# One fp32 transformer pair on one core: residual merge a chunk earlier, ones matmuls inside half blocks, fewer table loads, ScalarE for the high parts of entry blocks

## What is computed

```python
# first block
mix = concatenate([y_pool, y_sb]) @ w_out
h = h + rms_norm(mix, g_mix_post)
m = square(relu(rms_norm(h, g_mlp_pre) @ w_up)) @ w_down      # 4096 wide
h = h + rms_norm(m, g_mlp_post)
h = h + sigmoid(h @ w_ple_gate) * rms_norm(p @ w_ple_proj, g_ple)
# second block; sh, sc, g are columns of c_act @ w_ada + b_ada
x = h
x = x + g_m * hybrid_mixer(modulate(rmsnorm(x, norm_mix_g), sh_m, sc_m))
x = x + g_f * conv_ffn(modulate(rmsnorm(x, norm_ffn_g), sh_f, sc_f))   # silu(gate)*val @ w_down, 2816 wide
out = rmsnorm(x, norm_final_g)
```

## Time and profile before

| | us |
|---|---|
| median of 3 runs | 3202.91 |
| lowest, highest | 3197.24, 3203.24 |
| profiled execution, own time | 3209.44 |
| its span in the trace | 3207.7 |
| PE busy | 2999.0 (93%) |
| DVE, POOL, ACT busy | 1600.0, 1056.6, 796.3 |

### The profile page before, as it was taken

How to read it: one execution, slowest core, us unless ns; L and a number is a source line. 1 busy time by engine, 2 the same in 40 slices (tenths; PEclk the granted TensorE clock), 3 DMA queues, 4 the chain that set the end, 5 groups by cost and what they waited for, 6 DMA issues and landing times. The chain is left out here.

```text
span 3207.7 us, 34389 instructions
## 1 busy us (share of the span) xinstructions
PE 2999.0 (93%) x13294; PEld 2380.5 (74%) x13294; DVE 1600.0 (50%) x1598; ACT 796.3 (25%) x1066; POOL 1056.6 (33%) x476
## 2 busy tenths in 40 slices
PE   6999998999999998989999796799998999999996
PEld 5876576788888886768887564677786888888885
DVE  3639946545555557741300566555546433343337
ACT  2138843211222113220021234133213111111112
POOL 2330032444444442433343211310243343343441
PEclk9999999999999999989999697789999999999998
DMA  2121031122232222121122330200321111111111
GB/s 104 52 67 27 3 143 46 53 91 93 92 105 92 93 91 92 40 100 51 54 109 95 86 74 30 63 14 14 142 95 44 48 46 52 46 46 52 46 47 64
DMA packets 69593, 216.37 MB, mean 67 GB/s; under 512 B 9088, under 2 KB 15488, under 8 KB 68736
## 3 DMA queue, kind: packets, MB, share of 16 engines
q1 hardware_dynamic: 65616, 200.48, 19.6%
q10 hardware_dynamic: 3888, 14.68, 1.1%
HBM read 170.50 MB, written 22.54 MB: 60 GB/s over the span
## 5 line engine op out<-in xcount | busy, mean ns | idle before, releaser
L278 POOL TENSOR_TENSOR w_hi<-w_raw,inv_count 128x1024 fp32r<-128x1024 f32 x202 | 389.9, 1930 | 1780.3 <-PE ps L303 1113.2
L281 POOL TENSOR_TENSOR w_lo<-w_raw,w_hi 128x1024 fp32r<-128x1024 f32 x202 | 533.1, 2639 | 15.9
L303 PE MATMUL ps<-x_hi,w_hi 128*128 128x512 f32 x1216 | 378.7, 393 | 16.0 <-POOL w_lo L281 9.9
L303 PE MATMUL ps<-x_lo,w_hi 128*128 128x512 f32 x1216 | 377.1, 391 | 0.0
L303 PE MATMUL ps<-x_hi,w_lo 128*128 128x512 f32 x1216 | 377.0, 391 | 0.0
L303 PEld LDWEIGHTS ps<-x_hi,w_hi 128*128 128x128 f32 x1216 | 230.2, 190 | 65.9 <-issue 11.9
L303 PEld LDWEIGHTS ps<-x_lo,w_hi 128*128 128x128 f32 x1216 | 230.3, 189 | 48.3
L303 PEld LDWEIGHTS ps<-x_hi,w_lo 128*128 128x128 f32 x1216 | 229.9, 189 | 48.2
L303 PE MATMUL ps<-hidden_hi,w_hi 128*128 128x512 f32 x800 | 247.6, 391 | 11.7 <-DVE residual L2955 11.7
L303 PE MATMUL ps<-hidden_hi,w_lo 128*128 128x512 f32 x800 | 247.2, 390 | 0.0
L303 PE MATMUL ps<-hidden_lo,w_hi 128*128 128x512 f32 x800 | 247.2, 390 | 0.0
(11 more groups left out here) (399 smaller groups left out, 5078.5 us busy)
## 6 DMA issues: line engine op xcount, KB each, us to landing
w_raw<-wall SPq DMA_DIRECT2D x221, 512.0 KB, 3.5
ada_raw<-wada SPq DMA_DIRECT2D x48, 512.0 KB, 4.2
gates_scratch<-gate_out ACTq DMA_DIRECT2D x16, 512.0 KB, 2.6
gate_in<-gates_scratch SPq DMA_DIRECT2D x8, 1024.0 KB, 8.5
residual<-x_t SPq DMA_DIRECT2D x8, 512.0 KB, 8.6
residual<-x_t SPq DMA_DIRECT2D x2, 2048.0 KB, 9.6
emb_scratch<-emb_out ACTq DMA_DIRECT2D x8, 512.0 KB, 2.6
embedding<-emb_scratch SPq DMA_DIRECT2D x2, 2048.0 KB, 12.5
```

The lines of the kernel that those rows point to most:

```text
L278: nc.gpsimd.tensor_tensor(w_hi[:, slot, :], w_raw[:, slot, :], one.to_broadcast([P, S]), ALU.mult).then_inc(w_split, 1)
L281: nc.gpsimd.tensor_tensor(w_lo[:, slot, :], w_raw[:, slot, :], w_hi[:, slot, :].bitcast(F32), ALU.subtract).then_inc(w_split, 1)
L303: last = nc.tensor.matmul(ps[:, banks + c, :], lhs, x[:, k0 + k, c * HALF:(c + 1) * HALF], start=(left == nk * 3 - 1), stop=(left == 0))
```

## The change

1. **Merge** (mlp2_vector): the 8 instructions that add `acc2` to the residual move from behind `hidden` of the last chunk to in front of it, right behind the down sums of the chunk before; their wait on `pair_free` goes from 116 to 112.
2. **Ones matmul of half 0** moves from behind block (half 1, first of two) into it: behind its fourth tile in out1 and out2, behind its sixth in gate.
3. **Table loads**: three loads by hand are gone (start of mlp1, in2 and mlp2), one is put in gate behind the sigmoids of half 0. The last sigmoid piece of block GG + 6 and what hangs on it (`gate_last`, `gate_square`, `gate_add`, `gate_sum`) move from gate into in2.
4. **High parts**: for the first two blocks of mlp1, gate, in2 and mlp2 (8 blocks of 221), ACT makes w_hi (`split_high`) and POOL only w_lo (`split_low`).

```diff
+    def split_low(pool, b):
+        slot = b % 2
+        pool.wait_ge(w_split, b * 2 + 1)
+        nc.gpsimd.tensor_tensor(w_lo[:, slot, :], w_raw[:, slot, :],
+                                w_hi[:, slot, :].bitcast(F32), ALU.subtract).then_inc(w_split, 1)
+
+    def split_high(act, b):
+        slot = b % 2
+        act.wait_ge(w_landed[slot], 16 * (b // 2 + 1))
+        act.wait_ge(w_split, 2 * b)
+        act.wait_ge(w_used, b + 1)
+        nc.scalar.activation(w_hi[:, slot, :], w_raw[:, slot, :], ACT.Identity).then_inc(w_split, 1)
...
-    def last_two(pe, g0, x_hi, x_lo, job, between):
+    def last_two(pe, g0, x_hi, x_lo, job, between, at):
                 for k in range(8):
+                    if (c, u, k) == (1, 0, at):
+                        between()
                     last = half_step(pe, (g0 + u) % 2, x_hi, x_lo, k, 2 * u + c, c)
                 last.then_inc(half_full.sem if c == 0 else w_used, 1)
-                if (c, u) == (1, 0):
-                    between()
...
     def mlp1_scalar(act):
-        load_exp_ln()
...
         act_half_rstd(act, 0, 1)
         gain = lambda k: C1("g_mlp_pre", k)
+        split_high(act, GM)
         residual_high(act, 0, 0, gain)
...
         for k in range(1, 8):
             residual_high(act, k, 0, gain)
+            if k == 1:
+                split_high(act, GM + 1)
...
     def gate_scalar(act):
         square(11)
+        split_high(act, GG)
         for k in range(8):
             residual_high(act, k, 0)
             if k < 4:
                 square(12 + k)
+            if k == 3:
+                split_high(act, GG + 1)
...
     def in2_vector(dve):
         with before(GATE):
+            dve.wait_ge(*pair_free.at(7))
+            gate_add(dve, 6, 9, 1)
             dve.wait_ge(*pair_free.at(8))
             gate_add(dve, 7, 10, 1)
...
     def mlp2_vector(dve):
             down(4, 0)
-            hidden(*chunk_args(4, 1))
-            dve.wait_ge(*pair_free.at(116))
+            dve.wait_ge(*pair_free.at(112))
             for k in range(8):
                 nc.vector.scalar_tensor_tensor(out=res2[:, k, :], in0=acc2[:, k, :], scalar=ada_col(5, k),
                                                in1=res2[:, k, :], op0=ALU.mult, op1=ALU.add).then_inc(merged.sem, 1)
+            hidden(*chunk_args(4, 1))
             dve.wait_ge(*merged.at(8))
             down(4, 1, True)
```

More of the change, by code:

```diff
@@ L1083, in out1_pool @@
     def out1_pool(pool):
-        split_blocks(pool, GO + 2, GM + 1)
+        split_blocks(pool, GO + 2, GM)
+        split_low(pool, GM)
     def out1_scalar(act):
@@ L1214, in out1_tensor @@
                     pe.wait_ge(*pair_free.at(14 + u - 1))
-                last = out1_tiles((b + u) % 2, u, range(8), (c,), True, True)
-                last.then_inc(half_full.sem if c == 0 else w_used, 1)
                 if (c, u) == (1, 0):
+                    out1_tiles((b + u) % 2, u, range(4), (c,), True, False)
                     pe.wait_ge(*square_added.at(8 + 8))
                     half_stat(pe, 0).then_inc(stat_full.sem, 1)
+                    last = out1_tiles((b + u) % 2, u, range(4, 8), (c,), False, True)
+                else:
+                    last = out1_tiles((b + u) % 2, u, range(8), (c,), True, True)
+                last.then_inc(half_full.sem if c == 0 else w_used, 1)
     def out1_vector(dve):
@@ L1356, in mlp1_pool @@
     def mlp1_pool(pool):
-        split_blocks(pool, GM + 1, GM + 64)
+        split_low(pool, GM + 1)
+        split_blocks(pool, GM + 2, GM + 64)
     def square_sum(dve, n):
@@ L1606, in gate_pool @@
     def gate_pool(pool):
-        split_blocks(pool, GG, GI + 1)
+        split_low(pool, GG)
+        split_low(pool, GG + 1)
+        split_blocks(pool, GG + 2, GI)
+        split_low(pool, GI)
     def gate_square(act, k, c=None):
@@ L1663, in stat_0 @@
             half_stat(pe, 0).then_inc(stat_full.sem, 1)
-        last_two(pe, GG + 6, x_hi, x_lo, 6, stat_0)
+        last_two(pe, GG + 6, x_hi, x_lo, 6, stat_0, 6)
     def gate_sum(dve, k, n, c=None):
@@ L1756, in in2_pool @@
     def in2_pool(pool):
-        split_weights(pool, GI, 34)
+        split_low(pool, GI + 1)
+        split_blocks(pool, GI + 2, GI + 35)
     def in2_scalar(act):
@@ L1769, in in2_scalar @@
         with before(GATE):
+            gate_last(act, 0)
             gate_last(act, 1)
+        load_exp_ln()
+        split_high(act, GI + 1)
+        with before(GATE):
+            gate_square(act, 6, 1)
         high(2, 0)
@@ L1825, in in2_vector @@
         with before(GATE):
+            dve.wait_ge(*pair_free.at(7))
+            gate_add(dve, 6, 9, 1)
             dve.wait_ge(*pair_free.at(8))
             gate_add(dve, 7, 10, 1)
+        low(1, 0)
         scaled(2, 0)
-        low(1, 0)
+        with before(GATE):
+            gate_sum(dve, 6, 9, 1)
+        scaled(3, 0)
+        low(2, 0)
         with before(GATE):
             gate_sum(dve, 7, 10, 1)
-        for k in range(3, 8):
+        low(3, 0)
+        for k in range(4, 8):
             scaled(k, 0)
-            low(k - 1, 0)
+            if k > 4:
+                low(k - 1, 0)
         low(7, 0)
@@ L2671, in out2_pool @@
     def out2_pool(pool):
-        split_weights(pool, GY, 8)
+        split_blocks(pool, GY + 1, GN)
+        split_low(pool, GN)
     def out2_tensor(pe):
@@ L2787, in mlp2_pool @@
     def mlp2_pool(pool):
-        split_weights(pool, GN, 66)
+        split_low(pool, GN + 1)
+        split_blocks(pool, GN + 2, W_TOTAL)
     def final_square(act, n):
```

14 lines of the change are left out of this document (5 added, 9 removed).

## The result

The changed kernel takes 3183.08 us (median of 5 runs, 3178.80 to 3187.89) against 3202.91. The ratio is 0.9942 with a 95% interval from 0.9924 to 0.9961: 18.6 us faster, between 12.5 and 24.3. Forecast were 25.2 us and 3177.7; the time lies inside the stated range, and the gain is a quarter smaller than the sum. The profiled execution is the median one, with a span of 3181.3 us.

The account below looks back on a forecast made before the run. PE, busy 2999.0 of 3207.7 us, was taken as the bound, so only its stops and half clock pay. Terms of 14.7 + 1.0 + 1.5 + 7.0 + 1.0 = 25.2 us off the 3202.9 median gave 3177.7, range 3168 to 3188.

Parts of the forecast that it names:

- Term 1: Last chunk: moving the merge removes PE's stop and the half clock behind it; -14.7 us, between -13 and -15.5.
- Rival C: Last chunk: the merge meets POOL's weight passes and is not hidden, so PE waits; gain 14.5 us, 3188.4; chance 0.03.
- Term 4: Entry of in2: nothing stands before Ln any more, so Ln of half 1 comes earlier; -7.0 us, from -5 to -9.
- Terms 2 and 5: Entries of mlp1 and mlp2: earlier start, then held by second w_lo; -1.0 us each, to 0 or -2.7 and -2.2.
- Term 3: Entry of gate: PE starts 4.5 us earlier, then waits for the second block's w_lo; -1.5 us, from +0.3 to -3.4.
- B: Entries: later w_lo eats the gains; mlp1, gate, mlp2 give nothing, in2 only 3; gain 17.7 us, 3185.2; chance 0.17.
- A: Entries: shorter gaps bring the clock back to 2.4 GHz, each entry takes its outer value; gain 31.9 us, 3171.0; chance 0.17.
- D: Entries: first blocks fed in drips keep the clock at 1.2 GHz, kernel slower than before, 3207.7 us; chance 0.02.

Follow-up runs that it names:

- e2_no_merge: The changed kernel with the merge put back in its old place, all four entries as changed; 3198.96 us, ratio 0.9981.
- e4_gate_second_sooner: The changed kernel with one line moved: in gate's entry ScalarE makes the second block's high part after x_hi of tile 2, ahead of square 14; 3174.29 us, ratio 0.9914.
- e5_vector_low: On top of e4_gate_second_sooner, VectorE makes the second block's low part in all four entries, and mlp1's high part comes one tile sooner; 3180.54 us, ratio 0.9930.

## Why the prediction was right, and where not

- **Term 1, -14.7: right.** The changed kernel's trace gives 14.7 and the merge alone gives 14.7 by its trace and 15.0 by the ratio. Both traces are set against the same profiled execution before; against e2_no_merge's, where half clock behind the stop was shorter, it is 13.4, still inside the range of 13 to 15.5. The merge was slower than reckoned (16.05 us for 13.38) and so made the convolution later than the 2.3 us forecast: it ended at 3094.31, and the account puts the old start of that step, 3101.00, at 3089.34, so 5.0 us. It ended as forecast in the next idle time. Rival C was right that the merge would meet POOL's passes (2.7 us more) and wrong that PE would see it.
- **Term 4, -7.0: right in mechanism, a little large.** Three executions with these entries give -5.6 to -6.6, 6.2 in the mean. Less the account of -1.97, the forecast places were 1364.7 for tile 1 (1364.92 in the trace), 1369.5 for tile 2 (1369.68) and 1372.9 to 1375.8 for Ln of half 1 (1375.25). The clock took the slow end.
- **Terms 2 and 5, -1.0 each: -0.3 and -0.6 in the mean of three executions (+0.2 to -0.7, and -0.5 to -0.6).** PE starts as much sooner as said (2.7 us in mlp1 for 2.8, 3.1 in mlp2 for 3.2). The step that was off is who holds it afterwards: not PE's own wait for w_lo but a DVE instruction on the way to tile 1, which w_lo blocks (2.84 and 2.85 us). Among the signs, a wait for w_lo was to be PE's longest in mlp1 and mlp2; the rows name x_lo and y_lo, so that sign failed in both and came true in gate alone.
- **Term 3, -1.5: wrong, +0.2 to +0.5.** The places agree up to the hold (PE's first tile 4.9 us earlier, forecast 4.5; w_lo of the second block done at 1259.35, forecast 1260.9 less 2.04, so 0.5 late). The step that failed is the one behind: "five half steps of 0.68 us and two ones matmuls lead to Ln of half 1", 4.6 us at full clock and 6.5 with part of it at half. At full clock the same stretch took 5.53 (e4_gate_second_sooner), and 7.65 in the changed kernel. Five half steps are 3.4 us, so the working leaves 1.2 for the two ones matmuls. The rows show more. The first takes 0.46 us itself, but from the start of the matmul behind it to the next are 0.64 us instead of 0.23 at full clock (1266.46 to 1267.10) and 1.22 instead of 0.43 at half (1261.77 to 1262.99), so it costs 0.87 at full clock. Behind the second, which starts at 1266.01, Ln starts at 1267.06, 1.05 us later. Together 1.9 instead of 1.2. The rest is clock: the first two half steps with their ones matmul took 4.43 us (1259.41 to 1263.84) against 2.33 in e4_gate_second_sooner; from there to Ln both took 3.2.
- **The rivals.** B named the cause, the second block's w_lo, and its price was right for gate; for in2 it took away too much (3 left, 6.2 measured). By the total its 17.7 us are nearer to the measured 18.6 than the forecast's 25.2, which lies outside the interval of the gain. The time fell inside the stated range because that was drawn to take in B. A's half, the clock, was put as a gain that might come of itself with shorter stops (its value for in2 is 8.8 by the forecast's own places, not 8.9). It did not come: in all four entries half clock stood behind the last of the stops that were left (2.31, 4.50, 3.79 and 3.00 us), and with the clock kept up gate, in2 and mlp2 gave 2.1 + 1.6 + 1.5 us more. D never came near: these 5.2 us are far from the 25.2 that half clock would have had to cost.
- **The sum.** In the entries 6.8 us by the mean of the executions (0.3 + 6.2 + 0.6 less 0.3), where the forecast had 10.5. That is all that was missing: 14.7 + 6.8 = 21.5 (20.2 with the merge at 13.4), which the measured interval of 12.5 to 24.3 holds and the 25.2 of the forecast doesn't.
- **Against which execution.** Taking the differences off the median and not off the profiled execution was right: its own 3209.44 was 6.5 us above the median, and outside the four entries and the last chunk the other traces are 0.7 to 12.1 us shorter than it (difference of the spans less the sum of the table).

## What to carry to other kernels

When a wait at the start of a stage is taken away, look for the next block's preparation: it was hidden by that wait, and if it is queued in a fixed place on its engine it becomes the new stop; moving one line was worth 5.2 us in the trace, where all changes to the entries together had given 6.8. A stop of a few microseconds is paid twice where the clock falls behind it, so cheap work for PE in the stop can give back what no reordering does. And for terms of 1 to 5 us, compare one instruction's start in two traces stage by stage: the totals of the whole kernel scatter by more. Take several executions for that too: a single entry differed by up to 1.5 us between two executions of the same instructions.

## What the runs showed of the hardware

- Throwaway matmuls in the stops held the granted clock at 1.00 through gate, in2 and mlp2, where it was 0.83 to 0.89, and through mlp1 (0.83) in one of two executions; in the other it was 0.94. In gate PE went on at the same instant with them, by the account, as without.
- The same stop of 2.42 us, in code that both kernels share, was followed at once by half clock in two of the twelve traces here (the changed kernel and e5_vector_low) and by full clock in the other ten. Such places may account for the differences of up to 12.1 us between executions in untouched stages. What decides it in each was not tried.
- Behind a ones matmul (its operands are read as fp32, those of the products as fp32r) the next matmul runs 0.41 us longer from start to start at full clock, 0.8 at half, and the Ln that reads its result starts 1.05 us after it.
- A VectorE instruction that meets one of POOL's passes takes 2.83 to 2.86 us in the rows shown (2.45 to 2.89 over the changed kernel's four entries) instead of 0.68 to 0.75. POOL's w_lo of gate's second block itself takes 3.41 to 3.62 us; the other passes in the entries take 2.35 to 2.67.
- A load of ScalarE's function table took 1.28 us and was followed by the next instruction 0.01 to 0.02 us later where that one waited for nothing else, also where it switched to another set (1359.11 in the changed kernel).
